# First weights of the out and down projections split in the stage ahead, gain rows between the first steps, conv silu beside the up products

## What is computed

```python
# block 1
mod = c @ w_ada + b_ada                     # shift_m, scale_m, gate_m, shift_f, scale_f, gate_f
h = modulate(rms_norm(x, g_pre_mix), shift_m, scale_m);  proj = h @ w_in
y_a = sliding_window_attention(...);  y_m = sigmoid(o) * head_layer_norm(mlstm_chunkwise(...))
merged = sigmoid(g_a) * (y_a @ w_branch_attn) + sigmoid(g_m) * (y_m @ w_branch_mlstm)
x = x + gate_m * rms_norm(merged @ w_out, g_post_mix)                                  # out projection
h2 = modulate(rms_norm(x, g_pre_ffn), shift_f, scale_f)
x = x + gate_f * rms_norm((silu(h2 @ w_gate) * (h2 @ w_up)) @ w_ffn_down, g_post_ffn)  # down projection
# block 2
...                                          # retention and a sparse attention with top-k keys
x = x + rms_norm(mixed @ w_out_2, mix_norm_post_2)                                     # out projection
u = conv3(rms_norm(x, ffn_norm_pre_2) @ w_up_2)      # a causal depthwise conv of 3 taps on 2 x 2816 channels
x = x + rms_norm((silu(u[:, :2816]) * u[:, 2816:]) @ w_down_2, ffn_norm_post_2)        # down projection
```

## Time and profile before

| | |
|---|---|
| Runs of the kernel before | 3093.74, 3099.89, 3103.15 us |
| The profiled execution | 3097.24 us, of which the span (first to last instruction) 3095.5 |
| TensorE (PE) busy | 93% of the span |
| VectorE (DVE) | 42% |
| ScalarE (ACT) | 34% |
| GpSimd (POOL) | 32% |
| DMA | 230.24 MB, mean 74 GB/s |
| Mean granted TensorE clock | 0.972 of full speed |

### The profile page before, as it was taken

One profiled execution on the slowest core, in us unless ns is written; L12 is line 12 of the kernel. 1 busy time (PEld: TensorE's weight loads), 2 busy tenths in 40 slices (PEclk: granted clock), 3 DMA queues, 4 the chain that ended last, 5 costly groups with the idle time before them and its releaser, 6 DMA issues. The chain is left out here.

```text
span 3095.5 us, 36600 instructions
## 1 busy us (share of the span) xinstructions
PE 2871.5 (93%) x14048; PEld 2385.7 (77%) x14048; DVE 1298.7 (42%) x2088; ACT 1045.9 (34%) x1869; POOL 988.5 (32%) x668
## 2 busy tenths in 40 slices
PE   2999999999999999999998889869999999998998
PEld 2878888787788888878787677758878888886877
DVE  6646556322620000011746887554555233222143
ACT  3215545101520000012655676435443222222243
POOL 2001222423633333324641123420163333332454
PEclk9999999999999999999999899889999999998999
DMA  4531111322311111123430122100151111111342
GB/s 182 195 109 28 28 39 55 102 72 95 130 62 47 48 52 50 41 95 96 159 115 1 41 89 82 35 1 1 44 174 55 48 47 48 51 50 69 101 148 91
DMA packets 196110, 230.24 MB, mean 74 GB/s; under 512 B 11656, under 2 KB 140808, under 8 KB 195976
## 3 DMA queue, kind: packets, MB, share of 16 engines
q1 hardware_dynamic: 195976, 228.44, 23.0%
HBM read 203.24 MB, written 25.17 MB: 74 GB/s over the span
## 5 line engine op out<-in xcount | busy, mean ns | idle before, releaser
L133 PE MATMUL psum<-sb_h_hi,sb_w_hi 128*128 128x512 f32 x1792 | 707.9, 395 | 14.6 <-POOL sb_w_lo L928 9.5
L135 PE MATMUL psum<-sb_h_hi,sb_w_lo 128*128 128x512 f32 x1792 | 700.4, 391 | 0.0
L134 PE MATMUL psum<-sb_h_lo,sb_w_hi 128*128 128x512 f32 x1792 | 699.7, 390 | 0.0
L1539 POOL TENSOR_TENSOR sb_out_lo<-sb_out_raw,sb_out_hi 128x512 fp32r<-128x512 f32 (+1 forms) x180 | 323.5, 1804 | 507.2 <-ACT sb_out_hi L1529 507.1
L133 PEld LDWEIGHTS psum<-sb_h_hi,sb_w_hi 128*128 128x128 f32 x1792 | 338.2, 189 | 87.1 <-POOL sb_w_lo L928 10.5
L133 PE MATMUL psum<-sb_out_hi,sb_a_hi 128*128 128x512 f32 x960 | 381.8, 398 | 17.9 <-DVE sb_a_lo L1534 9.5
L135 PEld LDWEIGHTS psum<-sb_h_hi,sb_w_lo 128*128 128x128 f32 x1792 | 337.7, 188 | 71.4
L134 PEld LDWEIGHTS psum<-sb_h_lo,sb_w_hi 128*128 128x128 f32 x1792 | 338.5, 189 | 68.0
L926 POOL TENSOR_SCALAR sb_w_hi<-sb_w_raw 128x1024 fp32r<-128x1024 f32 x97 | 102.8, 1060 | 892.1 <-PE psum L135 612.5
L134 PE MATMUL psum<-sb_out_lo,sb_a_hi 128*128 128x512 f32 x960 | 378.6, 394 | 0.0
L135 PE MATMUL psum<-sb_out_hi,sb_a_lo 128*128 128x512 f32 x960 | 378.2, 394 | 0.0
(11 more groups left out here) (395 smaller groups left out, 4245.3 us busy)
## 6 DMA issues: line engine op xcount, KB each, us to landing
sb_w_raw<-in_w_up SPq DMA_DIRECT2D x44, 512.0 KB, 3.8
sb_late_w<-in_w_ada SPq DMA_DIRECT2D x32, 512.0 KB, 4.9
sb_w_raw<-in_w_in SPq DMA_DIRECT2D x56, 256.0 KB, 3.0
sb_w_raw<-in_w_ffn_gate SPq DMA_DIRECT2D x22, 512.0 KB, 3.8
sb_w_raw<-in_w_ffn_up SPq DMA_DIRECT2D x22, 512.0 KB, 3.8
sb_out_raw<-in_w_ffn_down SPq DMA_DIRECT2D x22, 512.0 KB, 3.5
sb_out_raw<-in_w_ffn_down SPq DMA_DIRECT2D x44, 256.0 KB, 3.0
sb_out_raw<-in_w_down SPq DMA_DIRECT2D x22, 512.0 KB, 3.3
```

The costliest lines, as they stand in the source:

```text
L133: nc.tensor.matmul(out, stationary.hi, moving.hi, start=start, stop=False)
L134: nc.tensor.matmul(out, stationary.hi, moving.lo, start=False, stop=False)
L135: return nc.tensor.matmul(out, stationary.lo, moving.hi, start=False, stop=stop)
L1539: self.nc.gpsimd.tensor_tensor(w.lo, raw, w.hi.bitcast(F32), ALU.subtract).then_inc(self.w_lo, 1)
```

## The change

**First weights ahead.** Each of the four stages in front of a `Closing` loads the first 128-row slice of its weights (512 KB) as the last DMA of its queue and splits it on GpSimd as that engine's last work: in `recurrent_phase` as a further gate tile, in `Up` after its loop into the gate's weight slot (once the last gate product is done) with the low part in the buffer of the last raw up weights, in `spread_phase` at the end. `Closing` takes them as `first`: step 0 then has no load, no high half and no low half of weights, its activation tile goes to the other slot, and step 2 needs no wait for its slots.

**Order at the start.** VectorE splits the activations of step 0 before it makes the diagonal tiles. TensorE does six of the eight places of step 0, the gain rows, six places of step 1, and then the two last places of steps 0 and 1.

**Conv loop.** ScalarE does base, silu, base in each pair. VectorE does the gate's two taps, the up's two taps and the product of a pair, then the next pair.

The diff, cut (passing the new arguments along is left out):

```diff
 def recurrent_phase(...):
+            sp.wait_ge(split_done, 2 * KD - 1)
+            sp.dma_start(raw[:, :, :].rearrange("p k c -> p (k c)"), next_w).then_inc(w_got, 16)
...
                 branch_split(m)
+            gate_split(2 * KD)
 class Up:
+        self.next_w, self.next_lo = next_w, core.lay(raw_at + 4, "next_lo", [P, D], R32)
...
+        sp.wait_ge(self.split_done, 2 * FT + 1)
+        sp.dma_start(self.raw[:, 0].rearrange("p k c -> p (k c)"), self.next_w).then_inc(self.w_got[0], 16)
...
+        pool.wait_ge(self.w_got[0], 16 * (FT + 1))
+        pool.wait_ge(self.mm_done, 2 * FT + 1)
+        pool.wait_ge(self.split_done, 2 * FT + 2)
+        flat = lambda a: a.rearrange("p k c -> p (k c)")
+        split_tile(self.nc, pool, self.passed, self.hi_done, 2 * FT + 1, flat(self.raw[:, 0]), Pair(flat(self.w.hi[:, 0]), self.next_lo[:, :]), self.split_done)
+        pool.wait_ge(self.split_done, 2 * FT + 3)
... (act)
+                        if s == 0:
+                            act.wait_ge(self.taps_done, i * 2 + (j + 1))
+                            nc.scalar.activation(y[:, j, 0], y[:, j, 0], ACT.Silu).then_inc(self.silu_done, 1)
...
-            if self.conv:
-                for j in range(2):
-                    act.wait_ge(self.taps_done, i * 2 + (j + 1))
-                    nc.scalar.activation(y[:, j, 0], y[:, j, 0], ACT.Silu).then_inc(self.silu_done, 1)
... (dve)
-                for j in range(2):
-                    dve.wait_ge(self.base_done, i * 4 + (2 * j + 2))
-                    for back in (1, 2):
-                        for s in range(2):
+            for j in range(2):
+                if conv:
+                    for s in range(2):
+                        dve.wait_ge(self.base_done, i * 4 + (2 * j + s + 1))
+                        for back in (1, 2):
...
-                    dve.sem_inc(self.read, 1)
-                    dve.sem_inc(self.taps_done, 1)
-            for j in range(2):
+                        dve.sem_inc(self.read if s else self.taps_done, 1)
 class Closing:
     def load(self, sp, u):
-        if u >= 2:
+        if u == 0 and self.first:
+            return
+        if u >= (3 if self.first else 2):
             sp.wait_ge(self.w_lo, self.slot_used(u))
+    def a_slot(self, u):
+        return 1 if u == 0 and self.first else self.at_step(u)[1]
     def split_high(self, act, u):
-        if u >= 2:
+        if u >= (3 if self.first else 2):
             act.wait_ge(self.k_done, self.slot_used(u))
         nc.scalar.activation(a.hi, src, ACT.Copy).then_inc(self.split_hi, 1)
+        if u == 0 and self.first:
+            return
     def split_w(self, pool, u):
+        if u == 0 and self.first:
+            pool.sem_inc(self.w_lo, 1)
+            return
     def pe(self, pe):
+        self.products(pe, 0, range(6))
         pe.wait_ge(self.diag_ready, KD)
...
         last.then_inc(self.gg_done, 1)
-        for u in range(3 * kt):
+        self.products(pe, 1, range(6))
+        for u in (0, 1):
+            self.products(pe, u, range(6, 8)).then_inc(self.k_done, 1)
+        for u in range(2, 3 * kt):
             self.step(pe, u)
     def dve(self, dve, ahead=None):
+        self.split_a(dve, 0)
         for k in range(KD):
             nc.vector.tensor_scalar(self.mix[:, 0, k * P:(k + 1) * P], ...).then_inc(self.diag_ready, 1)
-        self.split_a(dve, 0)
+        self.split_a(dve, 1)
         dve.wait_ge(self.gg_done, 1)
         nc.vector.tensor_copy(self.gg[:, :], ...).then_inc(self.gg_ready, 1)
 def spread_phase(...):
+                sp.wait_ge(k_used, (A_ + 1) * KD)
+                sp.dma_start(next_raw, next_w).then_inc(next_got, 16)
...
                 pool.wait_ge(top.marked, 2 * NP_)
+                pool.wait_ge(next_got, 16)
+                split_tile(nc, pool, passed, next_hi, 1, next_raw, next_first, next_done)
+                pool.wait_ge(next_done, 1)
 def block_kernel(...):
-        closing = Closing(core, dict(..., a=(FREE, FREE + 8), val=FREE + 96, x=(H, FREE + 64)),
+        closing = Closing(core, dict(..., a=(FREE + 96, FREE + 104), val=FREE + 4, x=(H, FREE + 64)),
```

77 lines of the change are left out of this document (45 added, 32 removed).

## The result

The changed kernel takes 3080.61 us in the median (3075.22 to 3088.21), the kernel before, on the same chip, 3100.78 (3093.74 to 3103.15): 20.2 us less, a ratio of 0.9938 with a 95% interval of 0.9924 to 0.9952. The profiled execution took 3079.02 us with a span of 3077.2, against 3097.24 and 3095.5: 18.3 us less in the span.

A forecast was written before the change was run, and what follows sets the result against it. TensorE, busy 2871.5 of 3095.5 us, was taken as the bound. Start and tail gains of 3.6 + 5.5 + 1.7 + 7.3 = 18.1 us off 3097.24 and 3099.89 gave 3079.1 and 3081.8; forecast 3080.5, range 3071 to 3092.

The forecast's parts named there:

- Restart: At each Closing start, step 0 needs only its activation tile, so TensorE resumes 1.4 us after the block's first L1527.
- Work to the end of step 1: At each start, 48 matmuls (10.85 us) plus gain rows at full clock (1.9): 12.75 us, then 0.3 to L1527.
- Clock: Each start resumes at half clock after the idle time that stays; costs 2.0 us, bounds 1.45 and 3.0.
- the second gap: TensorE's idle time after the gain rows, waiting for GpSimd's low half of the first weights; predicted to go.
- Gains by start: Time saved up to the end of step 1 at the four starts: 3.6, 5.5, 1.7 and 7.3 us, sum 18.1.
- the tail: Taps, silu and gating products behind the last matmul before the last start; the new conv order ends it 3.9 us earlier.
- The second fall: The clock's renewed drop behind the second gap, at the first start from 752.0 to 755.4; predicted to go with that gap.
- Table load: Possible ScalarE load before the base (Identity) behind a silu, on the last start's tail; bounds 0 and 1.28 us, taken 0.
- the lock between VectorE and GpSimd: Shared SBUF ports might let an added split hold up VectorE in the sparse stage; taken 0, bound 2.4 us, once.
- Step 1's weights hidden: At each start, step 1's weights are ready 8.0 us in, TensorE needs them at 8.9; cost 0, bound 1.0.
- rival (b): Waits only move, to step 1's low half or later block ends; 3083 to 3094 us; milder half in 0.16, harder in 0.13.
- Rival (d): Slower: conv loop's 10.7 us series outgrows TensorE's 21.7 per pair, each us above paid about 20 times; chance 0.03.

The follow-up runs named there:

- warm: Changed kernel plus matmuls doing no useful work at stage ends ahead of starts 1, 2 and 4, and ahead of the first product at all four; 3080.41 us, ratio 0.9944.
- warm_half: warm with step 1's weights copied and split in two halves of 512 columns; 3080.06 us, ratio 0.9938.
- swap: Changed kernel with the weights of steps 1 and 2 requested ahead of the next stage's weights; 3081.3 us, ratio 0.9939.
- conv_old: Changed kernel with the conv loop's old order (both silus after both tiles, all taps before both products); 3084.81 us, ratio 0.9952.
- third_plain: Changed kernel with its third start put back: no early load and split in the attention stage, old order there; 3085.12 us, ratio 0.996.
- before_conv: Kernel before with only the new conv loop order; 3095.42 us, ratio 0.9989.
- before_filled: Kernel before with four useless 128-column matmuls between the gain rows and step 0 at each start; 3096.06 us, ratio 0.9992.
- warm_swap: warm with the weights of steps 1 and 2 requested ahead of the next stage's weights; 3083.11 us, ratio 0.9953.
- warm_tail_half: warm_half without the six extra matmuls ahead of the first product; 3076.69 us, ratio 0.9929.
- rows_first: Changed kernel with early weights kept but the old order at the starts, gain rows before step 0; 3086.21 us, ratio 0.9956.

## Why the prediction was right

The time, 3080.61, is that of the forecast, 3080.5, and its mechanism is the one measured. Point by point:

- **Restart, 1.4 us behind the block's first high half.** 1.41 us at each of the four starts.
- **Work to the end of step 1, 12.75 us, and 0.3 to the next high half.** warm's fourth start and three of warm_half's, at full clock, take 14.4 to 14.5 us where the sum gives 14.45.
- **Clock, 2.0 us a start, between 1.45 and 3.0.** The four starts of the changed kernel less 14.45 give 1.6, 1.6, 2.1 and 1.8. This was in part luck of one execution: in swap, conv_old and third_plain the first start loses 2.7 to 2.8 and the second 2.5. With swap's starts the gain is 2.9 + 5.0 + 1.3 + 3.5 + 4.0 = 16.7 us, with the changed kernel's 19.3; the prediction's 18.1 lies between. The step that this touches is the mean of 2.0: I averaged stretches of unbroken work ahead of a rise, two of which came behind the second gap, and the first two starts usually lose more (two stretches of 3.4 us before cost 3.4; swap's single one, with 6.1 us of work, costs 3.05, so there nearly all of the first start's gain is the gap itself). The bounds held.
- **Gains by start.** Predicted 3.6, 5.5, 1.7 and 7.3 (with the tail), measured 4.0, 5.95, 1.6 and 7.7. conv_old and before_conv show the tail alone, third_plain the third start alone.
- **The second fall goes with the second gap.** No trace of a start without the gap has a second fall, and before_filled shows it from the other side: the gap filled, the fall gone, 1.6 us saved at the first start. The gap did not always bring one (before_conv's fourth start), so how much goes with it differs by execution.
- **Table load, 0 of at most 1.28.** The base stands 0.16 us behind the last matmul, with no load ahead of it; the conv loop's two lines have 11 loads each, as L1406 and L1414 had before. The groups of ScalarE, table loads in the conv loop:

```profile
L1422 ACT ACT_TABLE_LOAD x11 | 14.1, 1283 | 103.8 <-PE psum L135 103.8
L1426 ACT ACT_TABLE_LOAD x11 | 14.1, 1283 | 0.2
```

- **Nothing for the lock between VectorE and GpSimd, of at most 2.4.** In the attention stage the changed kernel's new split runs on GpSimd from 2087.55 to 2091.04, and VectorE's L2640, which reads PSUM and one SBUF tile, takes 0.56 us beside it, as it does ahead of it (at 2086.05). third_plain agrees: the stage is no shorter without the split, within its spread.

```profile
2088.68 2.36 POOL L928 TENSOR_TENSOR sb_next_lo<-sb_next_raw,sb_next_hi 128x1024 fp32r<-128x1024 f32 x1
2089.76 0.56 DVE L2640 CUSTOM_DVE_ANT_0 sb_scores<-psum,sb_bias 128x384 f32<-128x384 f32 x1 [0.56 <-PE psum L2591]
```

By the Trainium skill, "SBUF — State Buffer", the lock binds VectorE where it has two inputs in SBUF; no run here puts such an instruction beside the new split, so that half of the rule is untried.
- **Step 1's weights hidden.** I had 8.0 us for ready (its terms add to 7.9) and 8.9 for needed. They were ready at 752.04, 7.2 us in, and needed at 753.76, 8.9 us in. warm shows how thin that cover is: at full clock TensorE comes to step 1 some 7.3 to 7.6 us in, and waits 0.6 us at the second start, where the weights land 4.5 us in. There rival (b) was held off by the slow clock, and takes its place where the clock is mended; warm's 1.7 us at the first start are a later landing (5.6 us).
- **Rival (d), the series in the conv loop.** Windows, TensorE, inside that loop, 400 us without a gap, 0.226 us a matmul as in the earlier trace rows:

```profile
2400.00:2800.00 400.00, 400.00 (x1767) 331.20 (x1766) 116.05 (x92) 86.74 (x73) 125.65 (x73) 1.00 0.16 47
```

The sum missed what lies between the starts. From the first start to the second the kernel before has three stretches at half clock, in the part of the out projection where TensorE turns tiles between its products; the changed kernel has two. Windows of before, and then of the changed kernel:

```profile
816.90:820.30 3.40, 3.40 (x10) 2.62 (x9) 1.72 (x3) 0.43 (x1) 3.10 (x3) 0.51 0.88 274
833.90:837.30 3.40, 3.40 (x14) 2.92 (x13) 1.53 (x3) 2.59 (x4) 1.68 (x3) 0.50 0.00 0
882.00:885.40 3.40, 3.40 (x10) 2.60 (x9) 0.00 (x0) 0.00 (x0) 0.00 (x0) 0.55 0.00 0
```

```profile
814.80:818.20 3.40, 3.40 (x10) 2.62 (x9) 1.45 (x3) 0.17 (x1) 2.88 (x3) 0.50 0.82 246
831.80:835.20 3.40, 3.40 (x12) 2.82 (x11) 1.68 (x3) 2.57 (x4) 2.27 (x3) 0.51 0.00 0
835.20:1338.00 502.80, 497.72 (x2223) 412.21 (x2221) 52.75 (x51) 55.52 (x65) 159.21 (x106) 1.00 0.16 47
```

Each is 1.7 us, and they account for nearly all that the table shows in three of its columns. From the first to the second start: warm has one (575.7 us), the five kernels with early weights and no fillers two (577.2), as has warm_half (577.7 with its short wait), the three kernels without early weights, warm_swap and warm_tail_half three (578.8). From the third to the fourth, less the tail's 4.0 where it is long: none in the changed kernel, swap, conv_old and warm_tail_half (578.1), one in before, before_conv, before_filled, third_plain and warm (579.7), two in rows_first (581.3), three in warm_half and warm_swap (583.0).

The stretches do not come from nowhere. In all 12 traces TensorE has the same three waits for VectorE in the projection behind a start: 2.0 us some 52 us behind the start's end, 2.3 us at 69 to 70 and 2.3 to 2.4 us at 114 to 117. Each of the 41 stretches in these two columns begins between 0.2 us ahead of and 1.6 us behind the end of such a wait; the other 31 waits have none. The same wait in the changed kernel, where the clock stays at 1.00, and in rows_first, where it falls (the window at 2295.40 above):

```profile
2291.08 0.50 PE L133 MATMUL psum<-sb_out_hi,sb_a_hi 128*128 128x512 f32 x1 [2.05 <-DVE sb_a_lo L1559]
```

```profile
2293.66 0.50 PE L133 MATMUL psum<-sb_out_hi,sb_a_hi 128*128 128x512 f32 x1 [2.05 <-DVE sb_a_lo L1559]
```

Behind the last start there is one such wait, of 2.0 or 3.1 us: with 2.0 and no stretch the rest takes 242.7 to 242.8 us (before, before_conv), with 2.0 and one stretch 244.3 (the changed kernel, conv_old, warm_swap), with 3.1 and one 245.2 to 245.4 (five kernels), with 3.1 and one of twice the length 246.5 to 246.7 (rows_first, warm_half).

The other two columns are not accounted for: the part ahead of the first start takes 740.2 to 748.5 us, and 743.2, 743.8 and 748.5 in three kernels whose code is the same up to there (before, before_conv, before_filled); from the second start to the third it is 863.5 to 868.5. So against before, the changed kernel's execution has one stretch less at two places and one more at the third, and 1.6 and 1.1 us more in these two columns. The sum had none of this; that it came to 1.0 us in all, and the forecast so near, is luck.

## What to carry to other kernels

Where a block begins with the low half of weights that it fetches itself, let the stage ahead fetch and split them; count the gain as the second gap and the clock that it costs, and leave the first gap in the sum, because only the work changes and not the hand-over. Ask of each wait what comes next when it is gone: here it was step 1's weights, at one start hidden only by the slow clock. Stretches at half clock, 1.7 us each, come and go behind short waits far from the edit, so a single profile gives the mechanism and its floor, and only several give the size. Look at those waits too: the three of 2.0 to 2.4 us in each projection are paid in every kernel here, and a stretch behind more than half of them.
